# Hybrid DeltaNet/Conformer layer on one core: separate buffers for the next pair's inverse, weight rings of three, modulation in quarters

## The reference

```python
mod = silu(c) @ w_mod + b_mod                 # 6 x 2048 columns; the context has c_ctx
h  = modulate(rms_norm(x, w), sh1, sc1);  hc = modulate(rms_norm(ctx, w), sh1c, sc1c)
p  = h @ w_in;  pc = hc @ w_in[:, :STATE_END]
q, k, v, beta, g = delta_inputs(p, ...)       # depthwise conv of 5 taps, silu, l2 norm
# per head and chunk of 64 tokens, in both directions:
m = where(strict, (k*beta) @ k.T * decay, 0); t_inv = inverse(eye + m)
u = t_inv @ (v*beta);  w = t_inv @ (k*beta*exp(gcum))
attn = where(incl, q @ k.T * decay, 0)
v_new = u - w @ state;  o = q_dec @ state + attn @ v_new;  state = state*cd + k_dec.T @ v_new
mix = concat(rms_norm(o) * silu(z), conformer_branch(p[..., Z_END:]))   # conv of 31 taps, layer norm
x = x + g1 * rms_norm(mix @ w_out)
x = x + g2 * rms_norm(swiglu(modulate(rms_norm(x, w), sh2, sc2)))
```

## Time and profile before

| | us |
|---|---|
| median of 3 runs | 1681.26 (1679.15 to 1683.16) |
| profiled execution, own time | 1682.51 |
| its span in the trace | 1680.8 |

### The profile page before, as it was taken

The page is one execution under the profiler, slowest core; times in us unless marked ns, Lnnn a source line. Parts: engine busy times, 40 slices in busy tenths (PEclk is TensorE's granted clock), DMA queues, the critical chain, the costliest instruction groups (busy, mean ns, idle before and its releaser), DMA issues.

```text
span 1680.8 us, 25101 instructions
## 1 busy us (share of the span) xinstructions
PE 1557.9 (93%) x9317; PEld 1303.3 (78%) x9317; DVE 1031.7 (61%) x1436; ACT 768.9 (46%) x1035; POOL 231.3 (14%) x236
## 2 busy tenths in 40 slices
PE   3677999898989999999997999999999999999997
PEld 0356878787878888988876888888888888888785
DVE  1245878989796858575565555544444544777553
ACT  5446353534354655566344544444444444443342
POOL 2000232333232334335200000000000000000000
PEclk9899999999999999999998999999999999999999
DMA  9984645555555446554364466666666666888653
GB/s 358 400 305 154 197 133 182 195 176 176 196 181 163 148 142 192 161 195 143 126 213 150 139 188 190 190 190 190 188 189 189 190 190 200 319 309 314 200 187 113
DMA packets 182785, 334.58 MB, mean 199 GB/s; under 512 B 14706, under 2 KB 80354, under 8 KB 181793
## 3 DMA queue, kind: packets, MB, share of 16 engines
q1 hardware_dynamic: 182002, 330.89, 61.0%
q0 software_dynamic: 688, 2.39, 0.5%
HBM read 331.15 MB, written 2.10 MB: 198 GB/s over the span
## 4 chain that ended last, share of the span: by engine, by line
PE 74%; DVE 11%; DMA 6%; issue 4%; ACT 3%; POOL 1%; SPq 0%; DVEq 0%; ACTq 0%; POOLq 0%
PE PS L1717 62%; DMA first<-in_w_mod_dram 4%; DVE cacc L1575 3%; DVE w_lo L1297 3%; PE PS L1924 2%; DVE sil L1403 2%; PE PS L2017 2%; PE PS L1972 1%; PE PS L1723 1%; DMA raw<-in_w_in_dram 1%; PE PS L1914 1%; PE PS L1810 1%; PE PS L1872 1%; PE PS L1937 1%; PE PS L1827 1%
## 5 line engine op out<-in xcount | busy, mean ns | idle before, releaser
L875 ACT ACTIVATE w_hi<-raw 128x1024 fp32r<-128x1024 f32 x426 | 447.8, 1056 | 538.3 <-PE PS L1717 453.9
L1264 DVE TENSOR_TENSOR w_lo<-raw,w_hi 128x1024 fp32r<-128x1024 f32 x264 | 323.2, 1225 | 329.9 <-ACT w_hi L875 329.8
L1717 PE MATMUL PS<-w_hi,h_hi 128*128 128x512 f32 x704 | 274.8, 390 | 0.0
L1717 PE MATMUL PS<-w_hi,h_lo 128*128 128x512 f32 x704 | 274.0, 389 | 0.0
L1717 PE MATMUL PS<-w_lo,h_hi 128*128 128x512 f32 x704 | 274.0, 389 | 0.0
L1297 DVE TENSOR_TENSOR w_lo<-raw,w_hi 128x1024 fp32r<-128x1024 f32 x162 | 201.8, 1254 | 75.1 <-ACT w_hi L875 75.0
L1717 PE MATMUL PS<-h_hi,w_hi 128*128 128x256 f32 (+1 forms) x784 | 239.1, 305 | 1.8 <-DVE ub L1555 1.8
L1717 PE MATMUL PS<-h_lo,w_hi 128*128 128x256 f32 (+1 forms) x784 | 222.5, 284 | 0.0
L1717 PE MATMUL PS<-h_hi,w_lo 128*128 128x256 f32 (+1 forms) x784 | 222.4, 284 | 0.0
L1717 PEld LDWEIGHTS PS<-h_hi,w_hi 128*128 128x128 f32 (+1 forms) x784 | 149.6, 191 | 37.1 <-issue 27.9
L1717 PEld LDWEIGHTS PS<-w_hi,h_lo 128*128 128x128 f32 x704 | 132.1, 188 | 27.6
(11 more groups left out here) (314 smaller groups left out, 2373.1 us busy)
## 6 DMA issues: line engine op xcount, KB each, us to landing
raw<-in_w_in_dram SPq DMA_DIRECT2D x128, 512.0 KB, 3.9
raw<-in_w_mod_dram SPq DMA_DIRECT2D x96, 512.0 KB, 5.3
raw<-in_w_gate_dram SPq DMA_DIRECT2D x88, 512.0 KB, 3.7
raw<-in_w_up_dram SPq DMA_DIRECT2D x88, 512.0 KB, 3.6
raw<-in_w_down_dram SPq DMA_DIRECT2D x88, 512.0 KB, 4.3
first<-in_w_mod_dram SPq DMA_DIRECT2D x64, 512.0 KB, 9.7
raw<-in_w_out_dram SPq DMA_DIRECT2D x32, 512.0 KB, 4.3
gin<-in_w_mod_dram SPq DMA_DIRECT2D x32, 512.0 KB, 5.5
```

The lines of the kernel that those rows point to most:

```text
L875: act.activation(out_ap, in_ap, ACT.Copy).then_inc(S[kind], 1)
L1264: dve.tensor_tensor(w_lo[:, slot, :], raw[:, (R0 + n) % RING, :], w_hi[:, slot, :].bitcast(F32), ALU.subtract).then_inc(S["lo"], 1)
L1717: ins = pe.matmul(out_ap, a[i], b[j], start=start and n == 0, stop=stop and n == 2, skip_group_check=grouped)
```

## The change

1. **Buffers.** The rings `w_hi` and `w_lo` keep four places in memory, but the mixer uses three (`WR = 3`). In the fourth lie `mkl` and `kc`, and `gh`. `pi` has a buffer of its own. `kc` of the next pair waits only for this pair's last `mk`, `yone` waits no longer for `nx`; `mlo` no longer for `z`. The last `xadd` of a pair now waits for `nx` of the pair before.
2. **Queues.** The refinement leaves `solved` for a queue of its own, `fix` (`refined`). `AFTER` has a number per pair for each step: `z` 5 instead of 4 slots after `xadd`, `xy` mostly 2 instead of 1, `nr` 6 instead of 4, `yone` 5 instead of 2. `STREAM` is written out by hand; some latent projections change places.
3. **Splits ahead.** A split waits for the matmuls of the unit three before it; after a `zc` at most two units ahead.
4. **Modulation.** Four quarters in one bank (5) after one another. A DMA of `wm` still moves 512 KB: two rows of 512 columns instead of one row of 1024, so packets of 2 KB. `s1` runs four times, with five small operations instead of six. `EARLY` has four projections (k, v of the context, a, g) and three of their four units each: twelve units between the `wm` steps instead of six. They hold banks 0 to 3.
5. **Gates.** The second `ba` unit comes after `k` of the context's second pair, one projection sooner.

```diff
+WR = 3
-STREAM = [cu for n in range(NP) for cu in (("k", CTX, n), ("v", CTX, n), ("a", LAT, n), ("g", LAT, n))] + [
...
-GAP = {"solve": 2, "state": 3, "ready": 2}
+GAP = {"solve": 2, "fix": 2, "state": 3, "ready": 2}
...
-    ch.append(([("yone", (s, p))], [(AFTER["yone"], ("mk", (s, p, 0)))]))
...
+          ([("yone", (s, p))], [(AFTER["yone"][m], ("mk", (s, p, 0)))]),
...
+def refined(m):
+    both = [(*PAIRS[m], t) for t in range(NT)]
+    ch = [([("nr", o) for o in both] + [("nrr", o) for o in both],
+           [(AFTER["nr"][m], ("xadd", (*PAIRS[m], LEVELS - 1))), (AFTER["mlo"][m], ("mlo", both[1]))])]
...
-EARLY = [("k", CTX, 0), ("v", CTX, 0), ("a", LAT, 0)]
+NE = 4
+EARLY = STREAM[:NE]
+NQ = 4
+QT = NMOD // NQ
+MODB, MRB = 5, 3
...
         if kind == "zc":
-            split("hi", min(placed["hi"], current + AHEAD + 1))
+            split("hi", min(placed["hi"], current + AHEAD))
...
+            ov("w_hi_units", [WR, UN])
+            mkl = ov("mkl", [NT, 2, P], F32R)
+            kc = ov("kc", [NT, 2, P], F32R)
         w_hi = sb("w_hi", [RING, UN], F32R)
+            ov("w_lo_units", [WR, UN])
+            gh = ov("gh", [2, NT, 2, P], F32R)
         w_lo = sb("w_lo", [RING, UN], F32R)
...
-            split_before[u] = UNITS[n - RING] if n >= RING else None
+            split_before[u] = UNITS[n - WR] if n >= WR else None
...
-                        sp.dma_start(first[:, slot, :], w_mod_v[:, j, part * D + q * UN:part * D + (q + 1) * UN])
+                        sp.dma_start(first[:, slot, :].rearrange("p (a b) -> p a b", a=2),
+                                     w_mod_v[:, 2 * j:2 * j + 2, part * D + q * 512:part * D + (q + 1) * 512])
...
-                        need(pool, "nr", *PAIRS[PAIRS.index((s, p)) - 1], 1)
+                        need(pool, "mk", *PAIRS[PAIRS.index((s, p)) - 1], LEVELS - 1)
...
-                    need(pool, "z", s, p, LEVELS - 1)
...
-                    if (s, p) != PAIRS[0]:
-                        need(dve, "nx", *PAIRS[PAIRS.index((s, p)) - 1], 1)
...
+                    if (s, p) != PAIRS[0]:
+                        need(dve, "nx", *PAIRS[PAIRS.index((s, p)) - 1], 1)
```

More of the change, by code:

```diff
@@ L85, in solved @@
+MIX = {"ba0": 1, "ba1": 4}
 def solved(m):
     s, p = PAIRS[m]
[L88 to L93 removed]
@@ L252, in gates, with turn @@
         del mr[:n]
-    early = [(cu, g) for cu in EARLY for g in (0, 1)]
-    lat = turn_steps(0, LAT)
+    first_turns = [(s, kp) for kp in (0, 1) for s in (CTX, LAT)] + [(s, kp) for kp in range(2, 8) for s in (CTX, LAT)]
+    early, lat = [], []
+    def turn():
+        for t in first_turns[:2]:
+            plan.extend([("xT", t), ("xTc", t)])
+        del first_turns[:2]
     for n in range(NMOD):
+        q, at = divmod(n, QT)
+        if q and at == 0:
+            plan.append(("mrow", (q - 1,)))
+            turn()
         plan.append(("wm", (n,)))
@@ L275, in make_plan @@
             del lat[:3]
-    assert not early and not lat
+    assert not early and not lat and not first_turns
+    plan.extend([(k, (NQ - 1,)) for k in ("mrow", "modcol", "s1")])
+    plan.extend(turn_steps(NQ - 1, CTX))
+    lat = turn_steps(NQ - 1, LAT)
     done = 0
-    total = 4 * (len(STREAM) - 1) - 2 * len(EARLY)
+    total = 4 * (len(STREAM) - 1 - len(EARLY))
     for n, cu in enumerate(STREAM):
@@ L1188, in split @@
                 act.wait_ge(f_mm, mm_done)
-                copy(w_hi[:, (B0 + n) % RING, :], raw[:, (R0 + n) % RING, :], "hi")
+                copy(w_hi[:, place(n), :], raw[:, (R0 + n) % RING, :], "hi")
             def turned_hi(cs, c1):
@@ L1896, in _ @@
                     if (s, p) == PAIRS[0]:
-                        need(pe, "mrow", 1)
+                        need(pe, "mrow", NQ - 1)
+                        for r in first_read(held[INV]) if INV in held else []:
+                            need(pe, r[0], *r[1])
                     else:
```

226 lines of the change are left out of this document (122 added, 104 removed), and 4 rows, old and new, of the table AFTER.

## The result

The changed kernel takes 1695.73 us (median of 4 runs, 1693.85 to 1698.67) against 1681.08 (1679.15 to 1683.16) beside it: a ratio of 1.0082, 95% interval 1.0065 to 1.0099. It is slower by 0.8%, about 14 us, where 30 us less were forecast.

A forecast was written before the change was run, and what follows sets the result against it. TensorE, busy 93% of the span, was taken as the bound, with VectorE second. Terms -3.2 - 10 - 11 - 9 + 3 = -30.2 us took 1681.3 to 1651.1 us; forecast range 1636 to 1664 (0.58), 8 in 10 for 1628 to 1676.

The forecast's parts named there:

- The start: Loads up to the first dense unit: 9.2 and 5.4 us longer, less work behind them; net -3.2 us.
- six save 17.8 us: Six more dense units multiplied during the opening loads, 2.96 us each, shorten what follows by 17.8 us.
- 118 to 250 us (-10): Ramp after the loads: of 24.9 us idle time and lower clock, 10 come back through fewer bank and level waits.
- The chain (-11 and -9): Inverse's steps: longer distances cover TensorE's waits, winning 11 us from 250 to 525 us and 9 from 525 to 860.
- The clock: Three waits in the inverse's chain bring TensorE's clock down; 6.8 us of lower clock hang on them.
- VectorE as the limit from 250 to 525 us: VectorE, busy 246.6 of 275 us, limits the gain there: at 96% busy 257 us, of these 18 us only 11 taken.
- The rings (+3): Mixer's weight splits wait for a nearer unit with three ring places; cost taken as 3 us, bounds nothing to 55.
- The rival built on them: Splits make VectorE wait for weight copies in the mixer: slower, 1707 us; chance 0.08.
- The change doesn't overlap: Inverse's chain stays as long through new waits; only start, ramp and splits count: 1671 us; chance 0.18, shared with VectorE bound.

The follow-up runs named there:

- start alone: Kernel before with only the new start (modulation in quarters, four early projections), mixer tables and rings as before: ratio 1.0107, +18 us.
- mixer alone: Changed kernel with the old start (modulation in halves, three early projections, 16 slots before the gates): ratio 1.0121, +20 us.

## Why the prediction was wrong, point by point

**The start: timing as forecast, its worth not.** The last `wm` stands at 126.86 us (127 forecast) and the first dense unit behind it at 132.42 (132.5). With the queue full the loads moved at 378 GB/s (stretches 30 to 60 and 75 to 112), units of `w_in` in packets of 1 KB among them, and mostly at 380 to 391 where modulation in packets of 2 KB ran alone, the first half of this row:

```profile
GB/s 393 388 385 391 388 380 385 391 391 385 388 388 380 388 391 391 385 388 388 380 380 363 351 350 355 352 367 371 388 382 373 354 369 377 380 388 365 358 376 382
```

It is the changed kernel's row of DMA rates from 30 to 60 us; six loads of `w_in` are issued in it. The 384 GB/s worked out from the earlier trace rows holds. By the Trainium skill's figures (DMA: Bandwidth & Descriptors, "Why small descriptors are slow (HBM only)"), quoted in the prediction, it would be, as an estimate, 409 x 131 / 134 = 400 GB/s; the trace shows less. The error is in "six save 17.8 us". The 12th unit does start 15.8 us earlier (132.4 against 148.2), the 24th 8.8, the 36th 8.0, the 54th 5.5 us later, the 66th 8.4 later, the 114th 15.6 and the 158th 18.1 later. Part of that lead was never won: at the 24th unit the changed order has placed 2 of the 48 `mrm` steps and no level of the inverse, the old one 6 and four levels. What they cost, changed kernel, TensorE's groups from 118 to 596 us (busy us, mean ns, idle before):

```profile
L2073 PE MATMUL PS<-raw,csil 128*1 128x512 f32 x256 | 36.4, 642 | 2.8 <-DMA raw<-in_w_mod_dram 2.8
L1979 PE MATMUL PS<-gh,pi 128*128 128x128 f32 x120 | 28.7, 277 | 0.0
L1979 PE MATMUL PS<-pi,gh 128*128 128x128 f32 x120 | 28.2, 273 | 13.8 <-ACT pi L921 13.7
L1969 PE MATMUL PS<-gh,mkl 128*128 128x128 f32 x120 | 17.3, 268 | 1.4 <-issue 1.4
```

Eight matmuls are one `mrm`, 1.14 us; four, four and four are one level. The two groups of `xy` alternate and overlap, so their 28.7 and 28.2 us don't add up: together they are busy 31.7 us, and a level costs 1.06 + 0.58 = 1.64 us. Four of each are 11.1 us of postponed work, more than the lead of 8.8 us. I counted six units as saved and did not ask what had stood between them.

**118 to 250 us (-10): the opposite.** Units 12 to 36 take 140.3 us against 132.6, changed kernel and then before:

```profile
132.40:272.70 140.30, 120.16 (x876) 106.71 (x876) 102.93 (x193) 68.84 (x108) 25.96 (x24) 0.89 0.45 141
```

```profile
148.20:280.80 132.60, 119.94 (x935) 106.76 (x931) 99.64 (x175) 66.61 (x102) 36.41 (x32) 0.96 0.52 165
```

Idle 20.1 us instead of 12.7, clock 0.89 instead of 0.96: 7.5 us more of idle time and some 10 of missing clock, though three levels of the inverse and one `mrm` fewer are done. The wait for a bank (`sil`) fell only from 4.9 to 3.7 us, and the one for `sil` turned by TensorE is one of 4.7 us now.

**The chain (-11 and -9): the step that failed.** "The added distance of 0.7 to 2.2 us covers waits of 2.9 at most in nearly full." Two things are wrong in it. First, for `xy` and `seed` there was no added distance. I read "2 instead of 1" and "5 slots instead of 2" off the table `AFTER`; the two-slot gap of the queue `solve` already kept `xy` two slots behind `z`, and `seed` is two slots behind `yone` in both plans (six in the first latent pair of the new one). The 5 is the distance of `yone` from the mask ahead of it. So 16.2 of the 26.9 us of waits were to be covered by a distance that did not grow. Second, I priced a distance by TensorE's slots alone, as if the step waited for began when its own input was ready. The copy that `xy` waits for is issued at `xy`'s own slot, behind what ScalarE was given in the slots between, and in the new order more of that falls there: the copy starts 1.4 us behind `z` instead of 0.5. The waits rose from 8.0 to 17.6 us. Moving the copy, and with it some splits but no distance, took them to 2.9 us (shown). `pi` stood behind depthwise rows and a `w_lo`, 1.6 to 3.6 us and 1.2 us, in VectorE's order; `seed` waited 9.7 us instead of 8.2, and taking most of the rows out took the wait to 1.7 us (shown). Where the distance did grow the sentence holds: `nr` from 4 slots to 6, `nx` from 2 to 4 (10.7 us gone, 0.7 left).

**The clock** was taken as a gift that comes with the waits, 6.8 us. It is half of the mixer's price: 15.6 us of missing clock beside 14.6 us of idle time, with 15 stretches at half clock instead of 7.

**VectorE as the limit from 250 to 525 us**, "96%": it is busy 240.9 us there, 88%, not more than before. "An engine in order never comes to 100%" is no reason for the 96 either: TensorE is busy 400.00 of 400 us in the earlier trace rows. ScalarE, busy 112 of 275 us, did not look like a limit at all, and it is the larger part of the change's loss. Its share of busy time says nothing on where its runs fall.

**The rings (+3):** nothing (0.9983 to 1.0019). The rival built on them, the only slower one that I had (0.08), named the right sign, and its own sign in the profile is there: ScalarE's `w_hi` waits for TensorE through the mixer (75.9 us, 39 times, from 118 to 860 us in the changed kernel). It is not the cause.

**The rivals.** "The change doesn't overlap" is false, the `nr` and `nx` waits went. What I lacked is a rival for a step that is issued behind other work on its engine though its input is ready. That start and mixer interact (+18, +20, +14) is open in detail: the runs show that the place of the chain against the stream of units moves the time by 18 us with no distance changed (start alone), and two slots of the key norms by 17, not why each costs what it does. Of the 5 us that the early copy leaves, 3 are what the same edit costs the kernel before. The new plan also has 13 slots with no dense part in them, twelve of them in a row near the 40th unit, where the plan before and that of the start alone have none; no run tests what they cost.

## What to carry to other kernels

Read a distance off the finished order, not off the table that asks for it: here another rule had set it already. And two matmuls with a copy between them need more than slots between them: look at what the copying engine is given ahead of the copy, and issue the copy with its producer if its reader waits long. Before reading a start that is earlier as time won, count what has been postponed at the same unit. And try such an order with the side engines made light: if the change gains there and loses in full, the order of the small steps is a likely fault, and moving one of them ahead is the first thing to try, in both kernels: in the one before it cost 3 us.

## What the runs showed of the hardware

Long waits of TensorE often cost more than their length. In the mixers of before, after, start alone and mixer alone, 37 of 48 waits of 1.9 us or more stood within 3 us of a stretch at the lower level (4 of 7, 14 of 14, 12 of 13 and 7 of 14), but 8 of 38 of 1.0 to 1.9 us. Three of the seven such stretches before have no long wait beside them. Loads with the queue full ran at 409 GB/s in packets of 4 KB, mostly 380 to 391 in packets of 2 KB. Four depthwise instructions of VectorE took 1.5 us where GpSimd was idle, here in the changed kernel with the copy issued with `z`:

```profile
424.90 1.49 DVE L1626 SCALAR_TENSOR_TENSOR cacc<-ub,vcol,cacc 128x216 f32<-128x216 f32 x4
```

and over twice as long beside GpSimd's `mlo`, changed kernel, VectorE and then GpSimd:

```profile
512.15 3.57 DVE L1626 SCALAR_TENSOR_TENSOR cacc<-ub,vcol,cacc 128x216 f32<-128x216 f32 x4
```

```profile
512.31 2.83 POOL L877 TENSOR_TENSOR mlo<-mn,mhi 128x512 fp32r<-128x512 f32 x2 [2.10 <-ACT mhi L921]
```

The Trainium skill (SBUF — State Buffer, "SBUF: two separate sides") has it that a VectorE operation with two SBUF inputs and a GpSimd operation shut each other out of a port that they share; the trace agrees. These are the depthwise rows ahead of a `pi` (519.32 us) for which TensorE stood 3.3 us.
